# Two matrix products turned to tokens on partitions with 512 weight columns moving, in a two-layer hybrid encoder trunk

## The reference

```python
for i in range(2):
    h = rmsnorm(x, norm_mix[i])
    q, k, v, cglu, sc_b, sc_c, sc_h, gates = split(h @ w_in[i])
    y_a = window_attention(q, k, v, sinks, bias) @ w_attn_out[i]
    c = ca * sigmoid(cb)                        # ca, cb = halves of cglu
    c = causal_dwconv(c, conv_dw[i]) + bias     # 31 taps
    y_b = silu(layernorm(c)) @ w_conv_out[i]    # mean and variance over 1024 channels
    y_c = (sc_b * causal_dwconv(sc_c * sc_h, sc_conv[i])) @ w_sc_out[i]
    g = sigmoid(gates.reshape(b, s, 3, d))
    x = x + (g[0]*y_a + g[1]*y_b + g[2]*y_c) @ w_mix_out[i]
    h2 = rmsnorm(x, norm_ffn[i])
    x = x + (silu(h2 @ w_gate) * (h2 @ w_up)) @ w_down      # hidden width 2816
    x = x + (p[i] @ w_ple[i]) * sigmoid(rmsnorm(x, norm_ple[i]) @ w_ple_gate[i])
return rmsnorm(x, norm_final)
```

## Time and profile before

| | |
|---|---|
| median of 3 runs | 1159.49 us |
| the profiled execution's own time | 1159.33 us |
| its span, first to last instruction | 1157.4 us |
| instructions of PE, matmuls and weight loads each | 9266 |
| granted TensorE clock over the span | 0.998 of full speed |

### The profile page before, as it was taken

The page is one execution under the profiler, slowest core; times in us unless marked ns, Lnnn a source line. Parts: engine busy times, 40 slices in busy tenths (PEclk is TensorE's granted clock), DMA queues, the critical chain, the costliest instruction groups (busy, mean ns, idle before and its releaser), DMA issues.

```text
span 1157.4 us, 24058 instructions
## 1 busy us (share of the span) xinstructions
PE 1123.4 (97%) x9266; PEld 1102.4 (95%) x9266; DVE 833.7 (72%) x1253; ACT 708.4 (61%) x1143; POOL 420.3 (36%) x405
## 2 busy tenths in 40 slices
PE   5999899999999999999999989999999999999997
PEld 5998789999999999999989988999999999999997
DVE  6888997877667655455898899878776676545565
ACT  5768987767555543444666798877575554434445
POOL 0687568883002000002218876788610200000012
PEclk9999999999999999999999999999999999999999
DMA  8565334454553555455235544345545535545531
GB/s 310 190 232 196 110 117 157 167 206 164 186 212 114 191 209 211 155 184 215 110 136 199 212 146 140 117 146 195 197 169 187 207 112 216 213 155 185 210 146 38
DMA packets 29357, 201.54 MB, mean 174 GB/s; under 512 B 3520, under 2 KB 3712, under 8 KB 5840
## 3 DMA queue, kind: packets, MB, share of 16 engines
q1 hardware_dynamic: 27648, 195.38, 47.2%
q0 software_dynamic: 1088, 4.74, 1.2%
q10 hardware_dynamic: 528, 0.15, 0.1%
HBM read 199.19 MB, written 3.69 MB: 175 GB/s over the span
## 4 chain that ended last, share of the span: by engine, by line
PE 55%; DVE 15%; POOL 14%; ACT 8%; DMA 4%; issue 4%; POOLq 0%; DVEq 0%; ACTq 0%; SPq 0%
PE bank L328 17%; PE bank L329 17%; PE bank L330 17%; POOL pacc L1344 12%; DVE w_lo L908 5%; DMA w_raw<-in_wstream 4%; ACT w_hi L564 4%; DVE probs L1085 2%; POOL sqsum L1357 2%; ACT cprod L564 1%; DVE zacc L1109 1%; DVE act_lo L912 1%; PE bank L365 1%; PE bank L366 1%; DVE probs L1059 1%
## 5 line engine op out<-in xcount | busy, mean ns | idle before, releaser
L328 PE MATMUL bank<-h_hi,w_hi 128*128 128x256 f32 x1856 | 531.1, 286 | 2.8 <-DVE h_lo L912 0.9
L329 PE MATMUL bank<-h_lo,w_hi 128*128 128x256 f32 x1856 | 525.0, 283 | 0.0
L330 PE MATMUL bank<-h_hi,w_lo 128*128 128x256 f32 x1856 | 524.8, 283 | 0.0
L908 DVE TENSOR_TENSOR w_lo<-w_raw,w_hi 128x2048 fp32r<-128x2048 f32 x183 | 430.1, 2352 | 98.0 <-ACT w_hi L564 97.7
L564 ACT ACTIVATE w_hi<-w_raw 128x2048 fp32r<-128x2048 f32 (+1 forms) x185 | 351.3, 1901 | 153.8 <-DMA w_raw<-in_wstream 111.7
L328 PEld LDWEIGHTS bank<-h_hi,w_hi 128*128 128x128 f32 x1856 | 355.7, 192 | 10.8 <-issue 5.7
L329 PEld LDWEIGHTS bank<-h_lo,w_hi 128*128 128x128 f32 x1856 | 355.9, 192 | 0.1
L330 PEld LDWEIGHTS bank<-h_hi,w_lo 128*128 128x128 f32 x1856 | 355.8, 192 | 0.0
L1344 POOL TENSOR_TENSOR pacc<-pacc,cprod 128x256 f32<-128x256 f32 x280 | 303.9, 1085 | 76.9 <-ACT cprod L564 39.3
L328 PE MATMUL bank<-act_hi,w_hi 128*128 128x256 f32 x1024 | 291.9, 285 | 4.5 <-DVE w_lo L955 2.9
L329 PE MATMUL bank<-act_lo,w_hi 128*128 128x256 f32 x1024 | 290.3, 284 | 0.0
(11 more groups left out here) (145 smaller groups left out, 813.1 us busy)
## 6 DMA issues: line engine op xcount, KB each, us to landing
w_raw<-in_wstream SPq DMA_DIRECT2D x183, 1024.0 KB, 4.9
rel_bias_rows<-rel_bias_by_distance POOLq DMA_DIRECT2D x1, 2560.0 KB, 18.3
bias<-rel_bias_rows POOLq DMA_DIRECT2D x1, 1536.0 KB, 10.8
xs<-in_x SPq DMA_DIRECT2D x2, 512.0 KB, 4.5
w_raw<-in_wstream SPq DMA_DIRECT2D x2, 512.0 KB, 7.7
out_y<-xs SPq DMA_DIRECT2D x4, 256.0 KB, 2.4
zacc<-in_p POOLq DMA_DIRECT2D x2, 256.0 KB, 4.2
prms<-in_prm SPq DMA_DIRECT2D x1, 328.0 KB, 10.4
```

Source lines behind the costliest of these rows:

```text
L328: nc.tensor.matmul(o, wh, hi, start=first, stop=False, skip_group_check=True)
L329: nc.tensor.matmul(o, wh, lo, start=False, stop=False, skip_group_check=True)
L330: return nc.tensor.matmul(o, wl, hi, start=False, stop=last, skip_group_check=True)
L908: nc.vector.tensor_tensor(w_lo[:, n % RING, :], w_raw[:, n % RAW_RING, :], f32(w_hi[:, n % RING, :]), ALU.subtract).then_inc(lo_ready, 1)
```

## The change

- In the gate and output products of the three branches and in gate and up of the FFN the operands change places. `tok_group` has the activation block (128 features by 128 tokens) stationary and 512 weight columns moving, for two token tiles, into two banks of 512 columns. A group covers two chunks: 2 halves by 2 token tiles by 4 feature tiles by 3 matmuls, 48 in all.
- The branch results then have tokens on partitions. ACT and DVE work on 128 by 512 operands (`branch_gates`, `branch_product`), four times a branch each for sigmoid, product and, from the second branch on, sum. `turn_mix` transposes the mix on PE, in two halves of 8 tiles of 128 by 128 each.
- An FFN group holds 256 columns of gate and 256 of up. ACT takes the SiLU and DVE the product per token tile, and `turn_ffn` transposes the product with 4 transposes a group, one quarter into the next group.
- The FFN works on unnormalised `h_hi`/`h_lo` throughout; `mean_square_tokens` gives the mean of squares per token (6 products with one moving column), and its inverse root `rstd_tok` is the scale of the SiLU and of the product. `normalise_tiles` is left out for the FFN.
- The mean over channels is asked for after 4 chunks of `sc_out`, the variance after 7. `strips_late` has the first strips of `mix_out`, `down_a` and `down_b` do the early feature tiles first, and the last ones after the last transposes.
- The loops of PE, ACT and DVE in these sections are unrolled, and the weight stream holds the columns side by side (`side`).

```diff
+            def tok_group(L, s, c, src, bank, use, ready=None, amid=None, mid=None):
+                hi, lo, t0 = src
+                for half in range(2):
+                    slot = (c + half) % RING
+                    pe.wait_ge(lo_ready, L * CHUNKS + c + half + 1)
+                    for b in range(TB):
+                        rows, o = slice(b * P, (b + 1) * P), psum[bank + b][:, :]
+                        if half == 0:
+                            pe.wait_ge(bank_read[bank + b], use)
+                        for k in range(DT // 2):
+                            kt = half * DT // 2 + k
+                            wh = w_hi[:, slot, k * 512:(k + 1) * 512]
+                            wl = w_lo[:, slot, k * 512:(k + 1) * 512]
+                            if ready is not None and b == 0:
+                                ready(kt)
+                            nc.tensor.matmul(o, hi[:, t0 + kt, rows], wh, start=kt == 0, stop=False, skip_group_check=True)
+                            nc.tensor.matmul(o, hi[:, t0 + kt, rows], wl, start=False, stop=False, skip_group_check=True)
+                            mm = nc.tensor.matmul(o, lo[:, t0 + kt, rows], wh, start=False, stop=kt == DT - 1,
+                                                  skip_group_check=True)
+                        mm.then_inc(strip_done, 1)
+                        if amid is not None and half == b == 0:
+                            amid()
...
+            def strips_late(L, s, blk, src, ktiles, n, early, ready, amid, amid_at):
+                hi, lo, t0 = src
+                waited = -1
+                for part in (range(early), range(early, ktiles)):
+                    for e in range(n):
+                        bank = (s + e) % BANKS
+                        if part.start == 0:
+                            pe.wait_ge(bank_read[bank], L * USES + (s + e) // BANKS + 1)
+                            if e == amid_at:
+                                amid()
+                        for k in part:
+                            g = blk + e * ktiles + k
+                            if g // BPC > waited:
+                                waited = g // BPC
+                                pe.wait_ge(lo_ready, L * CHUNKS + waited + 1)
+                            if e == 0:
+                                ready(k)
+                            mm = mm3(bank, g, hi[:, t0 + k, :], lo[:, t0 + k, :], k == 0, k == ktiles - 1)
+                        if part.stop == ktiles:
+                            mm.then_inc(strip_done, 1)
...
-                def branch(name, i, src, ready, js=range(RING)):
-                    for j in js:
-                        s, blk = S0[name] + 2 * j, BPC * (C0[name] + j)
-                        strip(L, s, blk, h_src, DT, ds=2 * i, dc=RING * i)
-                        strip(L, s + 1, blk + DT, src, DT, ds=2 * i, dc=RING * i,
-                              ready=ready if j == 0 else None)
+                def branch(name, src, ready=None, js=range(4), amid=None, mid=None):
+                    for i in js:
+                        s = S0[name] + 4 * i
+                        tok_group(L, s, C0[name] + 2 * i, src if i % 2 else h_src, 2 * (i % 2), L * USES + (S0[name] + 8 * (i // 2)) // BANKS + 1,
+                                  ready=ready if i == 1 else None, amid=amid if i == 2 else None,
+                                  mid=mid if i == 3 else None)
+                def turn_mix(f):
+                    if f > 0:
+                        pe.wait_ge(mix_lo, L * 4 + 2)
+                    for b in range(TB):
+                        pe.wait_ge(mix_ready, L * 4 + 2 * f + b + 1)
+                        for e in range(4):
+                            t = 4 * f + e
+                            mm = nc.tensor.transpose(psum[6 + e // 2][:, e % 2 * SEQ + b * P:e % 2 * SEQ + (b + 1) * P],
+                                                     mix_tok[:, b, t * P:(t + 1) * P], idt[:, :])
+                    mm.then_inc(mix_turned, 1)
                 def tiles_ready(sm, base):
                     return lambda k: pe.wait_ge(sm, base + k + 1)
-                with pe.Fori(0, 2) as i:
-                    branch("attn_out", i, (act_hi, act_lo, 0), tiles_ready(attn_lo, L * QT))
+                branch("attn_out", (act_hi, act_lo, 0), tiles_ready(attn_lo, L * QT))
...
+                branch("sc_out", sc_src, tiles_ready(sc_lo, L * DT), js=range(2))
...
+                def variance():
+                    pe.wait_ge(csum_step, L * 2 * (DT - 1) + 2 * (DT - 1))
+                    nc.tensor.matmul(psum[4][:, 0:SEQ], ones[:, :], sqsum[:, :], start=True, stop=True).then_inc(cvar_done, 1)
+                branch("sc_out", sc_src, js=range(2, 4), mid=variance)
+                branch("conv_out", (act_hi, act_lo, 0), tiles_ready(conv_lo, L * DT), amid=lambda: turn_mix(0))
...
+                strips_late(L, S0["mix_out"], BPC * C0["mix_out"], (act_hi, act_lo, DT), DT, 4, 4,
+                            lambda k: pe.wait_ge(mix_lo, L * 4 + k // 2 + 1), lambda: turn_mix(1), 2)
+                plain("mix_out", DT, (act_hi, act_lo, DT), range(4, DT))
...
+                def turn_ffn(n):
+                    name, g = ("ffn_a", n) if n < GA else ("ffn_b", n - GA)
+                    if n >= 2:
+                        pe.wait_ge(ffn_lo, L * GROUPS + n - 1)
+                    for b in range(TB):
+                        wait_product(pe, L, name, g, b)
+                        for e in range(2):
+                            mm = nc.tensor.transpose(psum[6 + n % 2][:, e * SEQ + b * P:e * SEQ + (b + 1) * P],
+                                                     prod[:, b, e * P:(e + 1) * P], idt[:, :])
+                    mm.then_inc(ffn_turned, 1)
+                def mean_square_tokens(q):
+                    pe.wait_ge(sqsum_ready, q + 1)
+                    pe.wait_ge(sq_ready, 2 * q + 2)
+                    for b in range(TB):
+                        rows = slice(b * P, (b + 1) * P)
+                        nc.tensor.matmul(psum[4][:, b:b + 1], sqsum[:, rows], ones[:, 0:1], start=True, stop=False)
+                        nc.tensor.matmul(psum[4][:, b:b + 1], sq_last[0][:, rows], ones[:, 0:1], start=False, stop=False)
+                        mm = nc.tensor.matmul(psum[4][:, b:b + 1], sq_last[1][:, rows], ones[:, 0:1], start=False, stop=True)
+                    mm.then_inc(ms_ready, 1)
+                def ffn_stage(name, n0, n):
+                    for g in range(n):
+                        tok_group(L, S0[name] + 4 * g, C0[name] + 2 * g, h_src, 2 * (g % 2),
+                                  L * USES + S0[name] // BANKS + 2 * (g // 2) + 1,
+                                  ready=unscaled_ready(L * 2 + 1) if n0 == g == 0 else None,
+                                  amid=(lambda: turn_ffn(n0 + g - 1)) if g > 0 else None,
+                                  mid=(lambda: mean_square_tokens(L * 3 + 1)) if n0 == g == 0 else None)
+                def down_stage(name, ktiles, n0):
+                    strips_late(L, S0[name], BPC * C0[name], (act_hi, act_lo, 0), ktiles, 2, ktiles - 2,
+                                lambda k: pe.wait_ge(ffn_lo, L * GROUPS + n0 + k // 2 + 1),
+                                lambda: turn_ffn(n0 + ktiles // 2 - 1), 1)
+                    plain(name, ktiles, (act_hi, act_lo, 0), range(2, DT))
+                ffn_stage("ffn_a", 0, GA)
+                down_stage("down_a", FA, 0)
+                ffn_stage("ffn_b", GA, GB)
+                down_stage("down_b", FB, GA)
...
-                def branch_gates(name, u0, j, partner, chunk=True):
-                    activate(u0 + j, S0[name] + 2 * j, ACT.Sigmoid, partner)
-                    if chunk:
-                        after_chunk(C0[name] + j - 1)
+                def branch_gates(name, j):
+                    if j % 4 != 1:
+                        return
+                    s = S0[name] + 2 * (j - 1)
+                    for b in range(TB):
+                        wait_strip(act, L, s + 2 + b)
+                        if name == "attn_out" and j == 1:
+                            for t in (DT - 2, DT - 1):
+                                g = S0["sc"] + 3 * t + 1
+                                wait_read(act, L, g, g % BANKS)
+                        else:
+                            act.wait_ge(bank_read[2 + b], L * USES + s // BANKS + 1)
+                        nc.scalar.activation(gate_tok[b], psum[b][:, :], ACT.Sigmoid).then_inc(bank_read[b], 2)
+                def round_mix(f):
+                    act.wait_ge(mix_turned, L * 2 + f + 1)
+                    for e in range(2):
+                        t = DT + 4 * f + 2 * e
+                        copy(act_hi[:, t:t + 2, :].rearrange("p a b -> p (a b)"), psum[6 + e][:, :]).then_inc(mix_hi, 1)
...
+                def ffn_gates(name, n0, n):
+                    for g in range(n):
+                        s, c = S0[name] + 4 * g, C0[name] + 2 * g
+                        if n0 + g > 0:
```

(51 more changed lines are left out.)

265 lines of the change are left out of this document (106 added, 159 removed).

## The result

| | before | after |
|---|---|---|
| time, us: median (lowest to highest) | 1159.51 (1159.46 to 1159.73), run beside it | 1149.43 (1149.08 to 1150.77), 4 runs |
| profiled execution: time, span, granted clock | 1159.33, 1157.4, 0.998 | 1149.08, 1147.3, 0.996 |
| instructions | 24058 | 19188 |

What follows compares the result with a forecast made beforehand. PE, busy 97% of the span, was taken as the bound. From 1159.3, less 54.1 for wide matmuls, plus 13.2 for transposes and 5.5 for POOL stalls, came 1124 us; range 1116 to 1138.

Steps and rivals of the forecast that it cites:

- What bounds the kernel: PE, busy 97% of the span, never waits in the touched sections; their time is matmuls times 0.120 us.
- The wide matmuls: Branches, gate and up: 2208 matmuls of 512 columns at 0.2155 us instead of 0.240 save 54.1 us.
- rival 2: Every rounded matmul keeps a fixed 12 ns, so a wide one costs 0.228 us: 1145 us; chance 0.05.
- That speaks against the change: Wide matmuls by the skill's N/2.4 + 2.5 ns: only 6 us saved, time about 1172; set aside for measured rows.
- The transposes: Mix and FFN: 120 transposes in PE's stream at 0.110 us each cost 13.2 us in full.
- Removed normalisation, mean of squares: Dropping FFN normalisation beside a PE that doesn't wait, and mean-of-squares products at 1.32 us for 1.29: worth nothing.
- Waits for the turned results: PE's transposes of branch and FFN results find them ready: 0 taken, up to 5 us kept.
- Where a stall goes: POOL: PE waits for unchanged POOL before mean and variance: 1.25 + 1.5 us a layer, 5.5 us in all.
- Weights: Raw buffers supply a chunk every 4.6 us, PE wants one every 5.17 us: covered, no cost.
- 1: Three more POOL instructions a layer meet a `w_lo` before the mean or variance, 11.4 us: 1135 us; chance 0.14.
- 3: Rounded operands stream at 0.120 us per 256 columns, so wide matmuls take 0.240 us: 1172 us, slower; chance 0.05.
- 4: Transposes don't overlap, costing 0.27 us each instead of 0.11, 19 us more: 1143 us; chance 0.03.

Runs made afterwards that it cites:

- 2: The changed kernel with every 512-column matmul split into two of 256 columns: 1170.54 us, ratio 1.0085 to the kernel before.
- 3: The changed kernel with each FFN transpose done twice, 88 transposes more: 1156.88 us, ratio 0.9972 to the kernel before.
- run 7: The changed kernel without the third product (activation low times weight high) in `attn_out`: 1150.82 us, ratio 0.9916 to the kernel before.
- run 8: The changed kernel with a second block of unread matmuls of various shapes at its end: 64 and 128 moving columns took 110 to 114 ns each.

## Why the prediction was wrong

- **What bounds the kernel**: right for more work on PE: it stays at 97%, and work added to its stream lengthens the time (2 and 3). Less work shortens it only until POOL, ACT and DVE come late, which in `attn_out` and `sc_out` is at once (7).
- **"The wide matmuls"**: this step failed. It priced them at 0.2155 us, "the nearest row in streaming time", which is a full-precision pass, and read the 0.120 of the earlier trace rows as a near tie with a load not quite hidden. Measured is 0.2268: 13.3 ns that every rounded matmul pays at any width from 256 to 512. The term is 29.2 us instead of 54.1, which is 24.9 of the 25.4 us by which the forecast missed. This is rival 2, with its 0.228 us and 1145, to which I gave 0.05 because "full-precision passes show no such part". They don't, and they are another type: nearness in duration was taken for nearness in kind. With a price that only another type showed, 0.228 (the 12 ns kept) was an equal candidate to 0.2155, and the range should have held both. (The working writes the branches' matmuls as 3 x 2 x 576; it is 3 x 2 x 192 = 1152, and the 2208 used in the sum is right.)
- **"That speaks against the change"**: the rule of the Trainium skill that I set against it (TensorE: Matmul & The Clock Gate, Back-to-back issue gap) holds here for BF16, 109 and 216 ns, and for neither width of rounded float32, 120 and 227. To prefer the measured 0.120 was right; but the figure that I put in its place at 512 columns was as good as the rule's own, and only the narrow end had been measured for this type. The 1172 us that I gave for the rule contain the 5.5 us of POOL's waits; without them it is 1159.3 - 6 + 13.2 = 1166.5.
- **"The transposes"**: right, 0.110 us each and fully on the path. The 275 ns of the Trainium skill (TensorE: Matmul & The Clock Gate, Part 4: PE-mode transpose) are near the duration of one alone, 0.27 us here, and not its price in a row.
- **"Removed normalisation, mean of squares"**: nothing, as forecast, as far as the sections show; it was not tried alone.
- **"Waits for the turned results"**: I took 0 with up to 5 us, and got 5.4 by sections, 6.2 by medians. The working compared a chunk's 1.9 + 2.35 us with 5.2, but let the chunk start at once. It starts when it has landed, and the product stands behind it on both engines. I had also put products and sums at "under 2 us" where DVE alone takes 2.74; begun with the end of the group (306.2) they would have ended at 309.0, 0.2 after PE asks (an estimate), so the chunk is most of the wait. For the FFN's first group I had overlooked the table load before the SiLU.
- **"Where a stall goes: POOL"**: 5.5 us forecast, none came, since PE asks for the mean at 261.6 and not 257.65. POOL's sum for the mean did not stay put either: it ends at 257.41, 1.7 us earlier than before. With a PE as fast as forecast the waits would have been there: run 7 has 0.7 us before the mean and 3.5 before the variance, beside my 1.5 with an upper bound of 4. That 5.5 us forecast for POOL stand against 5.4 us of waits at the turns is luck; only because of it is the miss nearly equal to the one term of the wide matmuls.
- **Weights**: covered, as forecast, for the matmuls of the changed kernel. In run 7 PE waits 4.0 us for `w_lo` in layer 0, because ACT's queue holds the chunk up and not because the raw buffers are too few.
- **Rivals** 1, 3 and 4 did not occur.

## What to carry to other kernels

Price a new instruction shape from rows of its own type, or from a sweep of a dozen of them, and where only another type has a row, keep every constant that the old shape shows as a bound. Before placing a dependent step "n us later", list what stands in the producer's queue ahead of it and when that work's own input arrives, since the cover has to hold a transfer too. And a gain on a full engine is worth only what the next chain leaves: here that is 0.3 us before the variance.

## What the runs showed of the hardware that I had not expected

- A matmul of rounded float32 costs columns/2.4 + 13.3 ns (120, 147, 173, 227 ns at 256, 320, 384, 512; 448 takes 206.5), one of BF16 columns/2.4 + 2.5 ns.
- Going between rounded float32 and BF16 costs 17 ns a pair.
- Fewer stationary columns shorten a rounded matmul of 256 columns from 120 to 113 ns.
- Waits of PE of 2.2, 3.5 and 3.6 us were followed by 3.4 us at the 1.2 GHz level, with wide matmuls 0.43 us apart; another wait of 2.2 us was not (run 7). The clock also fell without any wait, behind matmuls of 64 and 128 moving columns 110 to 114 ns apart (run 8).
